# Down projection in seven block products per fold, with the weight and token sums on Pool

## What is computed

```python
h = rms_norm(x, ffn_norm_g[layer])
u, v = jnp.split(h @ w_up[layer], 2, axis=-1)
u = causal_dwconv(u, conv_w[layer], conv_b[layer])
x = x + (jax.nn.gelu(u) * v) @ w_down[layer]
return rms_norm(x, final_norm_g)
```

## Time and profile before

| | us |
|---|---|
| median of 3 runs | 2787.44 |
| lowest, highest | 2785.82, 2788.94 |
| the profiled execution, its own time | 2786.82 |
| its span, first to last instruction | 2785.0 |

### The profile page before, as it was taken

How to read it: one execution, slowest core, us unless ns; L and a number is a source line. 1 busy time by engine, 2 the same in 40 slices (tenths; PEclk the granted TensorE clock), 3 DMA queues, 4 the chain that set the end, 5 groups by cost and what they waited for, 6 DMA issues and landing times.

```text
span 2785.0 us, 40443 instructions
## 1 busy us (share of the span) xinstructions
PE 2751.5 (99%) x15873; PEld 2418.2 (87%) x15873; DVE 1503.3 (54%) x1819; ACT 1006.2 (36%) x1229; POOL 188.5 (7%) x156
## 2 busy tenths in 40 slices
PE   8999999999999999999999999999999999999998
PEld 6888888888888888888889999999999997888887
DVE  4445542223333333342488878888787864555554
ACT  4334432222223322132455444555544442122123
POOL 0003310000110100000000000000000010000002
PEclk9999999999999999999999999999999999999999
DMA  6432223333333233334434343534344444333332
GB/s 176 131 104 56 60 76 91 101 95 99 84 97 83 81 101 90 106 113 144 141 110 123 105 132 102 134 103 129 108 121 116 114 153 164 121 121 123 118 105 106
DMA packets 421653, 308.90 MB, mean 111 GB/s; under 512 B 6453, under 2 KB 367558, under 8 KB 420953
## 3 DMA queue, kind: packets, MB, share of 16 engines
q1 hardware_dynamic: 415335, 295.83, 36.6%
q10 hardware_dynamic: 5826, 10.76, 1.1%
q0 software_dynamic: 432, 1.50, 0.2%
HBM read 288.09 MB, written 22.06 MB: 111 GB/s over the span
## 4 chain that ended last, share of the span: by engine, by line
PE 93%; DVE 2%; ACT 2%; issue 1%; DMA 1%; SPq 0%; POOL 0%; DVEq 0%; ACTq 0%; POOLq 0%
PE bank L907 31%; PE bank L545 20%; PE bank L547 20%; PE bank L546 19%; PE bank L737 2%; PE bank L731 1%; DMA x_in<-in_x_dram 0%; DMA a_dram<-v_sb 0%; ACT l_win L1113 0%; ACT l_slc L1113 0%; PE bank L787 0%; DVE ring_lo L1755 0%; POOL l_slc L2004 0%; SPq L373 0%; DMA d_raw<-in_w_down_dram 0%
## 5 line engine op out<-in xcount | busy, mean ns | idle before, releaser
L907 PE MATMUL bank<-hl,ring_hi 128*128 128x256 f32 x2752 | 498.8, 284 | 4.2 <-issue 2.1
L545 PE MATMUL bank<-hl,w_hi 128*128 128x512 f32 x1248 | 494.0, 396 | 2.8 <-DVE w_lo L1452 2.8
L547 PE MATMUL bank<-hl,w_lo 128*128 128x512 f32 x1248 | 487.0, 390 | 0.0
L546 PE MATMUL bank<-hl,w_hi 128*128 128x512 f32 x1248 | 486.6, 390 | 0.0
L907 PEld LDWEIGHTS bank<-hl,ring_hi 128*128 128x128 f32 x2752 | 430.4, 192 | 4.6 <-issue 4.5
L907 PE MATMUL bank<-hl,ring_lo 128*128 128x256 f32 x1376 | 390.1, 284 | 0.0
L1442 DVE TENSOR_TENSOR w_lo<-w_raw,w_hi 128x2048 fp32r<-128x2048 f32 x107 | 245.2, 2292 | 265.2 <-ACT w_hi L1015 264.9
L1015 ACT ACTIVATE w_hi<-w_raw 128x2048 fp32r<-128x2048 f32 x107 | 204.6, 1912 | 435.3 <-PE bank L547 431.3
L547 PEld LDWEIGHTS bank<-hl,w_lo 128*128 128x128 f32 x1248 | 234.5, 188 | 49.5
L545 PEld LDWEIGHTS bank<-hl,w_hi 128*128 128x128 f32 x1248 | 234.7, 188 | 49.0 <-issue 3.3
L546 PEld LDWEIGHTS bank<-hl,w_hi 128*128 128x128 f32 x1248 | 234.8, 188 | 46.0
(11 more groups left out here) (292 smaller groups left out, 4212.1 us busy)
## 6 DMA issues: line engine op xcount, KB each, us to landing
w_raw<-in_w_in_dram SPq DMA_DIRECT2D x76, 1024.0 KB, 5.5
d_raw<-in_w_down_dram SPq DMA_DIRECT2D x44, 1024.0 KB, 5.1
raw<-in_w_up_dram SPq DMA_DIRECT2D x43, 1024.0 KB, 6.9
raw<-in_w_up_dram SPq DMA_DIRECT2D x86, 512.0 KB, 7.5
w_raw<-in_w_out_dram SPq DMA_DIRECT2D x16, 1024.0 KB, 5.1
a_dram<-v_sb SPq DMA_DIRECT2D x44, 256.0 KB, 2.1
a_in<-a_dram SPq DMA_DIRECT2D x11, 1024.0 KB, 7.4
w_raw<-in_w_branch_nsa_dram SPq DMA_DIRECT2D x8, 1024.0 KB, 5.3
```

Source lines behind the costliest of these rows:

```text
L545: mm(dst, l_hi, r_hi, start=first, stop=False)
L546: mm(dst, l_hi, r_lo, start=False, stop=False)
L547: return mm(dst, l_lo, r_hi, start=False, stop=final)
L907: last = mm(pb[bank][:, 0:TH], left[:, w], y[z][:, k, :], start=first and k == 0 and n == 0, stop=k == KH - 1 and n == 2, skip_group_check ...
```

## The change

Chunk 0, and two more chunks at the end, stay as they were (now `PLAIN` = 3, with `down_chunk(1)` and the tail as the second and third). The 4096 rows between them become four folds of 1024 rows. In a fold the weights are cut in two row halves of 512 and two column halves, `a` in two feature halves and two halves of 256 tokens. One unit is one fold by 1024 columns, so there are eight units n = 0 to 7, two for a fold. For a unit the products are

- P1 = Y11 X11, P2 = Y21 X12, P5 = T1 S1, P6 = T2 S2, P4 = T4 X22, P3 = Y22 S4, P7 = T3 S3

with weight sums S3 = X11 - X21, S2 = X22 - S3, S1 = S2 + X11, S4 = X12 - S2 and token sums T1 = a12 - a11, T3 = a22 - a12, T2 = a22 - T1, T4 = a21 - T2. Pool makes all of them. A weight sum is two instructions of 128x1024, a token sum one of 128x(4x256). The order of the products is P1, P2, P5, P6, P4 of the unit before, P3, P7, in all 56.

A product is 24 matmuls of 512 columns: 2 halves x 2 rows of 128 x 2 token tiles x 3. Its weight comes in two halves of 128x1024, each split into high (ACT, `fold_high`) and low (DVE, `fold_low`) in a ring of four. The split runs two products ahead: in the step of product i, DVE does the low of half 0 of product i+2, then the two additions of product i into `x1` (`fold_out`), then the low of half 1 of i+2. The seven token operands of a fold are split once (`y_high`, `y_low`, seven each): six of them in the steps of the odd unit before, behind the last use of the old one, and T4 in the even unit's.

The core of the diff:

```diff
-        with pe.Fori(0, 5) as i:
-            for par in range(2):
-                down_chunk(i * 2 + par, par, 8, i)
+        def fold_product(p, n):
+            ...
+            for h in range(2):
+                b = (2 * FOLD_AT[p, n] + h) % RING
+                pe.wait_ge(piece_ok, half_count(p, n, h))
+                for k in range(2):
+                    w = slice(k * 512, k * 512 + 512)
+                    for tt in range(2):
+                        tk = slice(tt * P, tt * P + P)
+                        for m, (z, right) in enumerate(((0, fold_hi[b]), (0, fold_lo[b]), (1, fold_hi[b]))):
+                            last = mm(pb[banks[tt]][:], y[:, z, 2 * h + k, tk], right[:, w],
+                                      start=first and h == 0 and k == 0 and m == 0, stop=h == 1 and k == 1 and m == 2,
+                                      skip_group_check=True)
+                last.then_inc(prod_done, 1)
+        down_chunk(0)
+        for p, n in FOLD:
+            fold_product(p, n)
+        down_chunk(1)
```

SP, the first loads and the loop over the units:

```diff
         sp.wait_ge(prod_done, PRODUCTS)
+        load_fold_a(0)
+        load_x11(0)
         for j in range(2, 4):
             sp.dma_start(x1[:, :, 512 * j:512 * j + 512], x1_d[:, :, 512 * j:512 * j + 512]).then_inc(x_loaded[j], 16)
+            sp.wait_ge(w_ready, S_DN + j + 1)
+            load_down(slot(S_DN + j), 0)
+        load_x12(0)
         store_a(unit(42))
         store_a(unit(43))
         sp.wait_ge(a_out, 16 * UNITS + 64)
+        load_x21(0)
+        load_x22(0)
+        ...
+        for n in range(FOLD_UNITS):
+            if n < FOLD_UNITS - 1:
+                sp.wait_ge(piece_ok, half_count("P5", n, 1))
+                load_x11(n + 1)
+            if 1 <= n < FOLD_UNITS - 1:
+                sp.wait_ge(piece_ok, half_count("P4", n - 1, 1))
+                load_x22(n + 1)
+            if n < FOLD_UNITS - 1:
+                sp.wait_ge(piece_ok, half_count("P3", n, 1))
+                load_x12(n + 1)
+            if n < FOLD_UNITS - 2:
+                sp.wait_ge(piece_ok, half_count("P7", n, 1))
+                load_x21(n + 2)
+            if n % 2 == 0:
+                sp.wait_ge(y_part, y_count("T4", n // 2))
+                if n < FOLD_UNITS - 2:
+                    load_fold_a(n // 2 + 1)
```

ACT in the first chunk, and DVE's loop:

```diff
+        down_hi(slot(S_DN + 3))
+        y_high("T1", 0, (w_used, S_DN + 2 + 3))
+        y_high("T2", 0, (w_used, S_DN + 2 + 3))
+        y_high("T3", 0, (dn_add, 4 + 8))
+        fold_high("P2", 0, 1)
+        ...
+        for i, (p, n) in enumerate(FOLD):
+            if i + 2 < len(FOLD):
+                fold_low(*FOLD[i + 2], 0)
+            fold_out(p, n)
+            if i + 2 < len(FOLD):
+                fold_low(*FOLD[i + 2], 1)
+            ...
+            elif p == "P4" and n % 2 == 0 and n < FOLD_UNITS - 2:
+                y_low("T2", n // 2 + 1)
+            elif p != "P6" and n % 2 == 1 and n < FOLD_UNITS - 1:
+                y_low(Y_OF[p], (n + 1) // 2)
```

Pool:

```diff
+        def sum_x(s, n, h):
+            c = slice(1024 * h, 1024 * h + 1024)
+            if s == "S3":
+                pool.wait_ge(n0_in[0], 16 * 21 + 16 * n + 16)
+                pool.wait_ge(n1_in[n % 2], 32 * (21 + n % 2) + 16 * (n // 2) + 16)
+                G.tensor_tensor(x21[n % 2][:, c], x11[:, c], x21[n % 2][:, c], ALU.subtract).then_inc(s_add, 1)
+            elif s == "S2":
+                pool.wait_ge(s_add, sum_count("S3", n, h))
+                pool.wait_ge(x22_in[n % 2], 16 * (n // 2) + 16)
+                if n:
+                    pool.wait_ge(piece_ok, half_count("P6", n - 1, 1))
+                G.tensor_tensor(s_2[:, c], x22[n % 2][:, c], x21[n % 2][:, c], ALU.subtract).then_inc(s_add, 1)
+            elif s == "S1":
+                ...
+                pool.wait_ge(piece_ok, half_count("P1", n, 1))
+                G.tensor_tensor(x11[:, c], s_2[:, c], x11[:, c], ALU.add).then_inc(s_add, 1)
+            else:
+                ...
+                pool.wait_ge(piece_ok, half_count("P2", n, 1))
+                G.tensor_tensor(x12[:, c], x12[:, c], s_2[:, c], ALU.subtract).then_inc(s_add, 1)
+        sum_t("T1", 0)
+        sum_t("T3", 0)
+        for s in ("S3", "S2", "S1"):
+            sums_x(s, 0)
+        sum_t("T2", 0)
+        sum_t("T4", 0)
+        for n in range(FOLD_UNITS):
+            sums_x("S4", n)
+            c = (n + 1) // 2
+            if n == FOLD_UNITS - 1:
+                break
+            if n % 2:
+                sum_t("T1", c)
+                sum_t("T3", c)
+            sums_x("S3", n + 1)
+            if n % 2:
+                sum_t("T2", c)
+            sums_x("S2", n + 1)
+            if n % 2:
+                sum_t("T4", c)
+            sums_x("S1", n + 1)
```

More of the change, by code:

```diff
@@ L510, in _ @@
         sp.wait_ge(a_out, 16 * UNITS + 64)
[L512 to L520, removed]
-        for par in range(2):
[L523 to L529, removed]
+        load_x21(0)
+        load_x22(0)
+        sp.wait_ge(w_ready, S_DN + 2 + 3)
+        load_x21(1)
+        sp.wait_ge(w_ready, S_DN + 3 + 3)
+        load_x22(1)
+        for n in range(FOLD_UNITS):
[16 more added lines that the diff above has]
+                else:
+                    load_a(1)
+        sp.wait_ge(piece_ok, half_count("P7", FOLD_UNITS - 1, 1))
+        load_down(slot(S_DN + 4), 1)
+        sp.wait_ge(piece_ok, half_count("P4", FOLD_UNITS - 1, 1))
+        load_down(slot(S_DN + 5), 1)
+        for n in range(S_DN + 6, S_DN + 12):
+            sp.wait_ge(w_ready, n + 1)
+            load_down(slot(n), (n - S_DN) // 4)
+            if n == S_DN + 7:
+                sp.wait_ge(a_ok, 2)
+                load_a(2)
         for t in range(TOK):
@@ L972, in _ @@
         bank_d = (5, 6, 7, 0)
[L974 to L982, removed]
@@ L984, in down_chunk @@
-        def down_chunk(c, par, per=0, i=None):
-            pe.wait_ge(a_ok, c + 1)
-            for j in range(4):
-                down_slot(slot(S_DN + 4 * par + j, per, i), par % 2, c * 4 + j)
-        with pe.Fori(0, 5) as i:
-            for par in range(2):
-                down_chunk(i * 2 + par, par, 8, i)
-        pe.wait_ge(a_ok, CHUNKS)
+        def down_chunk(e):
+            pe.wait_ge(a_ok, e + 1)
+            for j in range(4):
+                s = slot(S_DN + 4 * e + j)
+                pe.wait_ge(w_ready, s.n + 3)
+                for t in range(TOK):
+                    pe.wait_ge(dn_add, 16 * e + 4 * j + t + 1)
+                    if e and j == 0:
+                        pe.wait_ge(fold_add, out_count("P3" if t < 2 else "P4", FOLD_UNITS - 1))
+                    for k in range(4):
+                        w, tk = slice(k * 512, k * 512 + 512), slice(t * P, t * P + P)
+                        last = three(pb[bank_d[t]][:], a_hi[e][:, k, tk], a_lo[e][:, k, tk], d_hi[s.par][:, w], d_lo[s.par][:, w],
+                                     k == 0, k == 3)
+                    last.then_inc(dn_done if t < TOK - 1 else w_used, 1)
@@ L1376, in _ @@
         act.wait_ge(prod_done, last.q + 6)
-        a_high(0, 0, 16)
+        a_high(0)
         taps(last)
@@ L1380, in _ @@
         act.wait_ge(prod_done, PRODUCTS - 2)
[L1382 to L1389, removed]
[L1390 to L1393 removed]
         def tail_high(j):
[L1396 removed]
+            s = slot(S_DN + 4 * (PLAIN - 1) + j)
             act.wait_ge(w_loaded[s.par], s.half * 16 + 16)
@@ L1913, in down_add @@
                 V.scalar_tensor_tensor(d, pb[(5, 6, 7, 0)[t]][:], rr[:, t:t + 1], old, ALU.mult, ALU.add).then_inc(dn_add, 1)
-        def down_chunk(c, par, per=0, i=None):
-            for j in range(4):
-                down_lo(slot(S_DN + 4 * par + j + 1, per, i))
-                if j == 1:
-                    a_low(c + 1, (par + 1) % 2)
-                if i is None and c == 0:
-                    dve.wait_ge(x_loaded[j], 32)
-                    dve.wait_ge(prod_done, PRODUCTS)
-                down_add(slot(S_DN + 4 * par + j, per, i), c, j)
         before = unit(UNITS - 1)
@@ new lines, in sums_x @@
+        def sums_x(s, n):
+            for h in range(2):
+                sum_x(s, n, h)
+        sum_t("T1", 0)
[19 more added lines that the diff above has]
+            sums_x("S1", n + 1)
```

296 lines of the change are left out of this document (230 added, 66 removed).

## The result

| | before | after |
|---|---|---|
| median, us (12 runs each) | 2787.26 | 2792.99 |
| lowest, highest | 2785.71, 2789.40 | 2790.08, 2795.61 |
| the profiled execution, own time | 2786.82 | 2791.49 |
| its span | 2785.0 | 2789.5 |

A forecast was written before the change was run, and what follows sets the result against it. PE was taken to bound the kernel now, the shared line of DVE lows and Pool sums the changed folds. Terms -43.5 + 45 + 2 + 2 + 2 = +7.5 on 2786.82 gave 2794.3, as median 2795; range 2772 to 2820.

The forecast's parts named there:

- PE's columns, -43.5: Down projection: 1344 matmuls replace 1536 at an unchanged pace, 43.5 us off if nobody keeps PE waiting.
- rival 2: Folds: Pool and DVE run beside each other without exclusion, so PE bounds the folds; 2746 us, chance 8%.
- Rival 5: Folds: less work but a dearer matmul pace, 0.24 us, half of the 18 us hidden; 2804 us, chance 4%.
- The exclusion: Folds: DVE and Pool instructions on SBUF operands exclude each other, bank additions stay out; a sum holds the line 2.33 us.
- Pool's price, 2.47: Folds: one Pool sum of 1024 columns takes 2.47 us (2.18 to 2.58), 20 sums 49.4 us a fold.
- The fold, 91: A walked fold takes 91 us, between floor 85.7 and ceiling 106; PE stops 15 us, three times, 45 in all.
- Rival 1: Folds: the DVE and Pool line is never idle, 28.5 us in place of 45; 2776 us, chance 17%.
- rival 3: Folds: sums fall behind DVE's second low, a fold takes 98.5, 67 us in place of 45; 2817 us, chance 16%.
- The first chunk, +2: First chunk: the stop before slot 2 goes, a 6.8 us stop before P2's second half comes; 2 us more.
- rival 4: First chunk: costs 8 us more, by T2 waiting longer in ACT's queue; 2803 us, chance 10%.
- Unit 0, +2 with the clock's +2: 2 us for unit 0 and unit 6's end, and 2 us for slow clock behind stops of over 4 us.
- The end, 0: Behind the folds: slots 4 and 5 and gfin load in time, tail unchanged; nothing (0 to 3 us).

The follow-up runs named there:

- e1: The changed kernel with Pool's 80 sums cut to 8 columns, waits kept, P6 reading raw x22, sums left out of the result: 2744.15 us.
- e8: The changed kernel with Pool's sums replaced by subtractions of two different operands on a scratch buffer, which nobody reads or awaits: 2789.48 us.
- e6: The kernel before, with only slots 2 and 3 loaded ahead of the stores of `a`: 2781.75 us, ratio 0.9975 to before.
- e4: The changed kernel with all sums after the first chunk moved from Pool to DVE: 2761.40 us, ratio 0.9907 to before.
- e5: The changed kernel with the low part of the slot behind the folds moved behind the additions of the last P7: 2789.72 us.
- e9: As e4, with the low part of the slot behind the folds also moved behind the last P7's additions: 2758.94 us, ratio 0.9899 to before.
- e7: The kernel before, with 75 unread Pool subtractions of 128x1024 (one operand read twice) added beside its down projection: 2782.29 us.
- e10: As e9, but Pool makes the four token sums of each later fold, DVE the 16 weight sums: 2763.98 us, ratio 0.9918 to before.
- e2: As e1, but every sum covers 512 of its 1024 columns in place of 8: 2742.50 us.
- e3: As e8, but each of Pool's unread scratch subtractions reads one operand twice: 2755.05 us.

## Why the prediction was right, point by point

**PE's columns, -43.5.** Held: e1 has the pace (0.226), no gaps, and 2744.15 where rival 2's working said 2746. Rival 5 is out.

**The exclusion.** Held, with its figures: lows 1.08 to 1.09 behind Pool's end, additions 0.75 at most, a full hold 2.33, DVE's queue order decides. Rival 2 is out, and e8 shows that the exclusion needs no engine that waits for Pool. The Trainium skill's rule of an exclusive lock, held for the whole instruction (SBUF — State Buffer, section SBUF: two separate sides), cited in the prediction, agrees with this trace: a low part behind a sum ends 1.08 to 1.09 after it.

**Pool's price, 2.47.** It is 2.39 to 2.40. In a fold that is 1.4 us less on Pool, close to the 1.3 by which the fold came out shorter than walked. The walk also took 1.40 for two additions, their recorded time; from start to start they are 1.32 (2573.07 to 2574.39), 1.1 us less in a fold. The measured 2.40 is nearer to 2.36, the estimate from the figure of the Trainium skill (GPSIMD Engine Reference, section 3.1, Elementwise), than to the line through the earlier trace rows.

**The fold, 91.** It is 89.7 (86.2 the first time), over the floor of 85.7 and well under the ceiling of 106. The stops walked, beside those measured: P6 1.6 and 0.8 (in two parts), P4 4.8 and 3.7, P1 3.2 and 1.5, P2 2.3 and 1.5, P5 2.4 and 1.8; P3's 0.2 is not there. Same places, same order, each a little shorter; they are 9.4 of the 13.5. Another 2.3 is mostly the clock behind the stop of 3.71: P4, P3 and P7 take 18.6 us from 2493.57 to the next stop, where 16.3 would do, and eight matmuls start 0.40 to 0.43 apart (granted clock 0.71 from 2493.5 to 2497). So the stop need not be over 4 us, as the prediction put it. The rest, 1.8, is no clock: behind the shorter stops it is granted in full (1.00 from 2512 to 2516). A stop is counted from the end of the last matmul, recorded with 0.39 us where the next one normally starts 0.227 behind it, and the second matmul behind a stop comes 0.08 to 0.11 late: some 0.24 for each of seven shorter stops. Rival 1 asked for 9.5 and rival 3 for 22.3 over PE's time, measured are 13.5: the order was as walked. The three folds cost 37.1 where 45 stood in the sum; 3.5 of the difference is the first fold, which starts with DVE less late.

**The first chunk, +2.** Wrong, it is -3.9. The step that failed is the second half of P2 at 2349 against a want at 2342.5. The stores landed at 2316.0 (2317 forecast), x21 at 2321.1 (2323), T2 left Pool at 2338.8 (2342), the low part was ready at 2346.0. And PE wanted it only at 2344.3, since chunk 0 ended at 2336.0, 2 later than I had it. The stop is 1.69, not 6.8. No step was far off, but all of them erred to the same side. ACT copied T2 at 2338.86, as soon as Pool had it, so rival 4 is out. e6 prices the other half of the term, the stop that goes, at 6: hit. In after a stop of 0.74 stays in chunk 0 (at 2314.12, for an addition that stands behind a low part of 4.49, held up by Pool's T3), which the prediction did not have; chunk 0 takes 45.3 us in e1 and e6 and 46.2 in after.

**Unit 0, +2 with the clock's +2.** Here is the second miss, of the other sign: unit 0 alone cost 10.1 behind the stop of 1.69. P3 of unit 0 stops for 4.92, and it doesn't wait for a weight but for DVE's additions of P5, which it follows into the same banks. In the other units P4 of the unit before stands between them; unit 0 has none. Ahead of those additions DVE is held twice by Pool's sums for unit 1, the second of S3 (ends at 2361.22) and the first of S2:

```profile
2358.88 3.42 DVE L2084 TENSOR_TENSOR y_T<-a,y_T 128x1024 fp32r<-128x1024 f32 x1
2362.22 3.37 DVE L2079 TENSOR_TENSOR fold_lo<-x,fold_hi 128x1024 fp32r<-128x1024 f32 x1
2365.51 1.40 DVE L2094 SCALAR_TENSOR_TENSOR x<-bank,st,x 128x512 f32<-128x512 f32 x2
```

The walk followed the waits for weights and left out those for banks. With the sums on DVE (e4) the same stop is 0.27. Behind the stop in after the granted clock is 0.50 (2366 to 2370), the lower level of 1.2 GHz, as in the earlier trace rows.

**The end, 0.** It was 3.67, outside my 0 to 3: the last P4 waits for the additions of P7, and these stood in DVE's queue behind `down_lo` of the next slot, which itself waits for a copy and a load:

```profile
2684.24 2.29 DVE L2070 TENSOR_TENSOR d_lo<-d_raw,d_hi 128x2048 fp32r<-128x2048 f32 x1 [2.87 <-ACT d_hi L1496]
2686.45 1.40 DVE L2094 SCALAR_TENSOR_TENSOR x<-bank,st,x 128x512 f32<-128x512 f32 x2
```

I had asked whether the loads come in time, and not what the early work stands in front of. e5 and e9 show it by moving one line. The move took 2.2 us off the stop in e5 (unit 7 is 2.1 shorter) and 1.0 off it in e9, against e4 (unit 7 is 1.0 shorter). The two additions, 1.5, stay in both.

**Sum.** 45 was 37.1 (7.9 too much), the first chunk was 5.9 too much, units 0 and 7 and the end 10.1 too little (14.1 against 4), and 0.7 in the stages ahead stood in no term. The total was off by 2 to 3 us since the errors have both signs. The sign is not due to the large terms either: -43.5 for the columns, +37.1 for the folds and -3.9 for the first chunk are -10.3, and only units 0 and 7, mostly by the two waits for banks that the walk did not have, make it a plus. With the 4 forecast for them the sum would be -5.6, or -2.1 if the first fold had then taken the 89.7 of the others. The mechanism was right; that the sign and the size of the total were right too is largely luck.

**What stays open.** Why the first chunk of e7 gains 4.3 us is argued from the order of the loads (the move of `gfin` is the only transfer that changed), and no run moves `gfin` alone. Nor was a Pool sum tried that is always placed behind a first low part; by e10 it would cost DVE 0.9 and save 1.135.

## What to carry to other kernels

When work goes to an idle engine that can't run beside the busy one (here Pool and DVE, each on SBUF operands), price it at what it takes from the busy one: Pool's 2.39 us sum held DVE for 0.9 to 2.3 us, and DVE needs 1.135 to do it itself. Count only against gaps that the busy engine really has: 75 shorter sums were free where DVE idled half the time (e7), half-length ones were free in the folds (e2), and the full ones, for which DVE had no gap left, cost 45 us (e8 against e1). In a walk, follow the waits for buffers and banks beside those for data, above all in the first and last round, where one of the usual steps is missing.

## What the runs showed beyond what was expected

- A Pool subtraction of 128x1024 that reads one operand twice takes 1.893 us, with two different operands 2.397; 0.5 us less Pool time a sum made 34 us of the kernel's (e3 against e8). Per fold it is all of it: 20 sums x 0.504 = 10.1, and units 3 to 6, two folds, take 159.2 us in e3 and 179.6 in e8.
- Where a Pool instruction is released by the end of a DVE instruction and DVE's queue is empty, DVE isn't touched (e7: low parts of 2.293 in the median and 2.295 at most; 2.292 and 2.294 in before).
- The 1 MB load of `gfin` that Pool issues among the first chunk's transfers seems to delay them by 2.9 us: SP asks for slot 2, behind the stores, at 2304.90 with it and at 2301.97 in e7 without it. At the 400 GB/s of the earlier trace rows its bytes are 2.6 us.
